# A decoder step on one core: cached keys turned in place by VectorE, two key buffers in turn, scores on 32x32 tiles

## The reference

```python
def dilated_attention_sample(q, k_new, v_new, cache_k, cache_v, rel_bias):   # cache: (8, 2048, 12, 64)
    kc = concatenate([cache_k, k_new], axis=1); vc = concatenate([cache_v, v_new], axis=1)
    for w, d in ((128, 1), (512, 4), (2048, 16)):
        idx = n_past + arange(n_new)[:, None] - arange(w // d + 1)[None, :] * d
        kg, vg = kc[:, idx], vc[:, idx]
        logits = einsum('bthe,btjhe->bhtj', q, kg) * 64 ** -0.5 + bias[bucket(j * d)]
        p, s, lse = softmax_stats(logits, idx >= 0)
        o = einsum('bhtj,btjhe->bthe', p, vg) / s
    return merge_branches(outs, lses)        # branches weighted by their softmax denominators
```

## Time and profile before

| | |
|---|---|
| median of 3 runs | 1428.6 us (1427.8 to 1431.9) |
| the profiled execution, timed | 1427.6 us |
| its span, first to last instruction | 1425.7 us |
| mean granted TensorE clock | 0.985 of 2.4 GHz |
| busy: TensorE, VectorE, ScalarE | 97%, 36%, 17% |
| DMA over the span | 524.8 MB, 368 GB/s |

### The profile page before, as it was taken

The page is one execution under the profiler, slowest core; times in us unless marked ns, Lnnn a source line. Parts: engine busy times, 40 slices in busy tenths (PEclk is TensorE's granted clock), DMA queues, the critical chain, the costliest instruction groups (busy, mean ns, idle before and its releaser), DMA issues.

```text
span 1425.7 us, 22384 instructions
## 1 busy us (share of the span) xinstructions
PE 1378.0 (97%) x7929; PEld 585.1 (41%) x7930; DVE 519.1 (36%) x1159; ACT 242.8 (17%) x432; POOL 24.3 (2%) x45
## 2 busy tenths in 40 slices
PE   5999999999989999999999999999999999999996
PEld 2655666665453333333333333333333333333332
DVE  2211356554674232333233332323332332323325
ACT  0001334443021111111111111111111111111111
POOL 0000000000030000000000000000000000000000
PEclk9999999999979999999999999999999999999998
DMA  9959457999948999999999988999999999998981
GB/s 361 372 204 350 174 182 304 417 419 379 349 142 319 399 422 418 427 426 424 427 427 426 426 364 371 414 425 427 425 425 425 428 426 425 424 425 322 419 346 37
DMA packets 62917, 524.78 MB, mean 368 GB/s; under 512 B 8732, under 2 KB 10325, under 8 KB 22762
## 3 DMA queue, kind: packets, MB, share of 16 engines
q1 hardware_dynamic: 58896, 517.61, 88.5%
q0 software_dynamic: 2160, 5.96, 1.2%
q10 hardware_dynamic: 1834, 0.84, 0.3%
HBM read 520.92 MB, written 3.46 MB: 368 GB/s over the span
## 4 chain that ended last, share of the span: by engine, by line
PE 81%; DMA 11%; issue 4%; DVE 2%; SPq 1%; ACT 0%; ACTq 0%; DVEq 0%; POOLq 0%
PE ps L1845 29%; PE ps L1925 14%; PE ps L1361 6%; DMA arena<-in_w_up 6%; PE ps L1783 5%; DMA arena<-in_cache_v 4%; PE ps L1737 3%; PE ps L1424 3%; PE ps L1652 3%; PE ps L1837 2%; PE ps L1594 2%; PE ps L1421 2%; PE ps L1741 2%; PE ps L1855 2%; DMA arena<-by_distance 1%
## 5 line engine op out<-in xcount | busy, mean ns | idle before, releaser
L1845 PE MATMUL ps<-arena 128*64 128x512 f32 x2048 | 451.3, 598 | 3.3 <-DMA arena<-in_w_up 3.3
L1845 PEld LDWEIGHTS ps<-arena 128*64 128x64 f32 x2048 | 144.3, 138 | 308.1 <-issue 300.2
L1925 PE MATMUL ps<-arena 128*64 128x512 f32 x1024 | 226.8, 595 | 0.1
L1361 PE MATMUL ps<-arena 128*128 128x128 f32 (+4 forms) x1071 | 151.8, 283 | 19.5 <-DVE arena L784 10.8
L1281 DVE TENSOR_SCALAR arena<-ps 128x512 f32<-128x512 f32 (+1 forms) x35 | 24.2, 691 | 367.6 <-PE ps L1845 306.1
L1361 PEld LDWEIGHTS ps<-arena 128*128 128x128 f32 (+4 forms) x1071 | 116.6, 144 | 82.4 <-issue 48.2
L1925 PEld LDWEIGHTS ps<-arena 128*64 128x64 f32 x1024 | 70.9, 137 | 150.2 <-issue 150.2
L727 ACT ACTIVATE arena<-arena 128x512 f32<-128x512 f32 (+1 forms) x35 | 22.1, 631 | 443.6 <-DVE arena L1281 443.6
L1216 DVE TENSOR_TENSOR arena<-arena,ps 128x512 f32<-128x512 f32 x32 | 22.1, 690 | 192.6 <-PE ps L1774 192.6
L1424 PE MATMUL ps<-arena 128*128 128x320 f32 x288 | 82.8, 439 | 1.9 <-DMA arena<-in_w_in 1.9
L1783 PE MATMUL ps<-arena 64*128 64x512 f32 x288 | 79.7, 637 | 0.0
(11 more groups left out here) (264 smaller groups left out, 979.8 us busy)
## 6 DMA issues: line engine op xcount, KB each, us to landing
arena<-in_w_up SPq DMA_DIRECT2D x128, 2048.0 KB, 15.7
arena<-in_w_down SPq DMA_DIRECT2D x128, 1024.0 KB, 13.5
arena<-in_w_ada SPq DMA_DIRECT2D x12, 2048.0 KB, 17.4
arena<-in_cache_k SPq DMA_DIRECT2D x16, 1536.0 KB, 14.4
arena<-in_cache_v SPq DMA_DIRECT2D x16, 1536.0 KB, 9.6
arena<-in_w_in SPq DMA_DIRECT2D x6, 2048.0 KB, 23.4
arena<-in_cache_k SPq DMA_DIRECT2D x32, 192.0 KB, 12.5
arena<-in_cache_v SPq DMA_DIRECT2D x32, 192.0 KB, 10.5
```

Source lines behind the costliest of these rows:

```text
L1361: return nc.tensor.transpose(o, i, ident[0:n, 0:n])
L1845: ins = mm(bank(part)[64 * h:64 * h + 64], xe_t[:, 0, at:at + 64], up_w[:, k, FF * part + 512 * h:FF * part + 512 * h + 512], start=False, ...
L1925: ins = mm(bank(3)[64 * h:64 * h + 64], a_t[:, 0, at:at + 64], dn_w[:, kk, 512 * h:512 * h + 512], start=kk == 0, stop=kk == KC - 1)
```

## The change

VectorE transposes the keys in place: one `transpose` of a part of the buffer turns each 32x32 square by itself (10 blocks x 24 squares along a partition). A square then holds 32 of the 64 values of a head in its partitions and 32 keys along them. TensorE multiplies 32x32 tiles: for each of 24 groups of 32 values and each of 4 quarters of the partitions, one product of 32 rows, 32 columns and 320 keys; four quarters go to four banks (0 to 3), three groups of heads to three column tiles. `q_wide` holds the queries for this, each at the partitions of all four quarters; they come from `q_rep`, made once by 16 small products with the identity (`qr_done`) and four copies on ScalarE (`qr_ready`). The scores of the new keys go to bank 4 as before, by `qbd`. The 60 transposes of a batch on TensorE, their 18 copies, and `kt_sb` are gone; in its place lies a second key buffer (`k_buf[0]`, `k_buf[1]`).

The keys of batch 0 are turned one block at a time at steps 4 to 13 of the loop over the prompt's heads, those of batch 1 around the table of biases, those of batch b+2 in `dve_batch` of b.

```diff
-        k_sb = view(KX, KB, DA)
...
-        kt_sb = view(KTX, AC, NCACHE)
+        k_buf = [view(KX, KB, DA), view(KTX, KB, DA)]
+        MX = KTX + KB * DA
+        FG = DA // 32
+        q_wide = view(MX, FG, 32)
...
+        q_rep = view(P, FG, NTOK - SEQ)
...
-            load_keys(ck, slice(1, 2), 0)
+            sp.wait_ge(proj_done, len(UNITS))
+            load_keys(1)
             sp.wait_ge(out_kv, 96)
             sp.wait_ge(sb_done, 1)
             sp.dma_start(wo_sb, wo_d).then_inc(wo_in, 16)
-            load_keys(ck, slice(2, 3), 1)
+            sp.wait_ge(s_done, 1)
+            load_keys(2)
             for b in range(1, NB - 1):
+                if b < NB - 2:
+                    sp.wait_ge(s_done, b + 1)
+                    load_keys(b + 2)
                 load_values(slice(b, b + 1), b)
-                if b < NB - 2:
-                    load_keys(ck, slice(b + 2, b + 3), b + 1)
...
+            act.wait_ge(vec_out, 64)
+            act.wait_ge(qr_done, 1)
+            for g in range(4):
+                ins = nc.scalar.copy(q_rep.rearrange("p (c g) t -> p g c t", g=4)[:, g],
+                                     bank(3 + g, 0, AC * 64).rearrange("p (c t) -> p c t", c=AC))
...
+            def turn_keys(par, js):
+                part = k_buf[par][:, js, :].rearrange("p j d -> p (j d)")
+                return v_.transpose(part, part)
+            def turn_group(par, group, times):
+                dve.wait_ge(k_low_in[par][group] if group < 2 else k_high_in[par], times * (16 if group < 2 else 64))
+                turn_keys(par, slice(4 * group, min(4 * group + 4, KB))).then_inc(k_ready, 1)
...
+            v_.memset(q_wide, 0.0)
...
+                for m in range(4):
+                    ins = v_.tensor_copy(wide[:, :, m, :, 8 * m:8 * m + 8],
+                                         q_rep.rearrange("p (j m h) t -> p j m h t", j=3, m=4)[:, :, m, :, own])
...
-            queries(slice(SEQ, SEQ + NS))
-
+            dve.wait_ge(qr_ready, 1)
+            queries(slice(SEQ, SEQ + NS), slice(0, NS))
+            turn_group(1, 0, 1)
             dve.wait_ge(sb_done, 1)
...
             mean_squares(0)
+            turn_group(1, 1, 1)
+            turn_group(1, 2, 1)
...
-                V(v_.tensor_tensor_reduce(prob[0:96, 0:NCACHE], ps[0:96, 0:NCACHE], s_bias[0:96, 0:NCACHE], 1.0, -3e38,
-                                          ALU.add, ALU.max, st[0:96, 12:13]))
-                V(v_.tensor_reduce(st[0:96, 13:14], prob[0:96, NCACHE:NCACHE + 64], AX.X, ALU.max))
+                for a in range(4):
+                    ins = v_.tensor_tensor_reduce(blocks[0][:, :, a], bank(a, 0, 32 * KB)[0:96].rearrange("p (j k) -> p j k", k=32),
+                                            blocks[1][:, :, a], 1.0, -3e38, ALU.add, ALU.max, st[0:96, 18 + a:19 + a])
+                V(ins)
+                V(v_.tensor_reduce(st[0:96, 22:23], prob[0:96, NCACHE:NCACHE + 64], AX.X, ALU.max))
+                V(v_.tensor_reduce(st[0:96, 12:13], st[0:96, 18:23], AX.X, ALU.max))
...
+                if turns:
+                    turn_group(par, 0, times)
                 dve.wait_ge(st_done, b * 3 + 2)
...
+                if turns:
+                    turn_group(par, 1, times)
+                    turn_group(par, 2, times)
...
+            dve_batch(NB - 2, 0, 0, False, True, False)
             inverse_roots(0)
...
+            def cached_scores(keys):
+                for n in range(FG // 3):
+                    for a in range(4):
+                        for j in range(3):
+                            f, rows = FG // 3 * j + n, slice(32 * a, 32 * a + 32)
+                            ins = mm(bank(a, 0, 32 * KB)[32 * j:32 * j + 32].rearrange("p (j k) -> p j k", k=32),
+                               q_wide[rows, f, :], keys[rows, :, 32 * f:32 * f + 32], start=n == 0, stop=n == FG // 3 - 1,
+                               tile_position=(32 * a, 32 * j))
```

More of the change, by code:

```diff
@@ L412, in _ @@
             sp.dma_start(query_sum[0:96], t["query_sum"].rearrange("p (a b) -> p a b", a=3)).then_inc(hot_in, 16)
-            def load_keys(cache, b, before):
-                for half in range(2):
-                    sp.wait_ge(kt_done, before * 18 + AC * half + AC)
-                    load_low(cache, k_sb, b, half, k_low_in[half])
-                sp.wait_ge(kt_done, before * 18 + 3 * AC)
-                load_high(cache, k_sb, b, k_high_in)
             def load_values(b, used):
@@ L969, in _, with queries @@
             V(v_.memset(place[:, CAP:128], -0.5))
-            def queries(cols):
+            def queries(cols, own):
                 for par in range(2):
@@ L1094, in dve_batch @@
                 if not first:
                     mask_output(b - 1)
-                if more:
-                    dve_turned(0, b + 1)
-                if not first:
                     keep_output(b - 1)
-                if more:
-                    dve_turned(1, b + 1)
-                    dve_turned(2, b + 1)
-                if first:
-                    queries(slice(SEQ + NS, SEQ + 2 * NS))
+                if turns:
+                    turn_group(par, 0, times)
                 dve.wait_ge(st_done, b * 3 + 2)
@@ L1557, in sums_of_squares @@
                 ins.then_inc(ss_done, 1)
+            pe.wait_ge(proj_act, len([w for w in UNITS if w[3] == "act"]))
+            for g in range(4):
+                for a in range(0, 128, 32):
+                    ins = mm(bank(3 + g, 0, AC * 64)[a:a + 32].rearrange("p (c t) -> p c t", c=AC),
+                             ident[:, 32 * g:32 * g + 32], q_t[:, :, SEQ:NTOK], start=True, stop=True, tile_position=(0, a))
+            ins.then_inc(qr_done, 1)
             pe.wait_ge(hot_in, 64)
@@ L1606, in output_sample, with pe_batch @@
                 ins.then_inc(wo_done, 1)
-            def pe_batch(b, first, more):
+            def pe_batch(b, par, first, more):
                 pe.wait_ge(qbd_ready, b + 1)
                 pe.wait_ge(s_max, b + 1)
-                pe.wait_ge(kt_dve, b * 9 + 10)
-                pe.wait_ge(kt_act, b * 9 + 10)
-                scores(bank(0), lambda c: kt_sb[:, c, 0:512])
-                scores(bank(1), lambda c: kt_sb[:, c, 512:1024])
-                scores(bank(2, 0, 256), lambda c: kt_sb[:, c, 1024:NCACHE])
-                scores(bank(2, 256, 320), lambda c: k_t[:, c, SEQ:NTOK]).then_inc(s_done, 1)
+                pe.wait_ge(k_ready, b * 3 + 3)
+                scores(bank(4, 0, 64), lambda c: k_t[:, c, SEQ:NTOK])
+                cached_scores(k_buf[par]).then_inc(s_done, 1)
                 if not first:
                     values(b - 1)
-                if more:
-                    keys(0, b + 1)
-                else:
+                if not more:
                     pe.wait_ge(og_ready, 1)
@@ L1627, in pe_batch @@
                     heads_apart(b - 1)
-                if more:
-                    keys(1, b + 1)
-                    keys(2, b + 1)
                 if not first:
```

156 lines of the change are left out of this document (50 added, 106 removed).

## The result

The changed kernel takes 1440.6 us (median; 1436.6 to 1443.1), against 1428.6 before: ratio 1.0074, interval 1.0059 to 1.0088. It is 0.7% slower, where 1423.0 was forecast. Its profiled execution has a span of 1441.4 us, the one of before 1425.7.

The account below looks back on a forecast made before the run. It took DMA to bound the loop, 18.5 us a turn, TensorE's 18.1 close behind. 8.1 us earlier at the stream's end less 2.5 for the clock gave 5.6: 1427.6 to 1422.0, median 1.0 above, 1423.0 us; range 1417 to 1436.

Parts of the forecast that it names:

- What bounds the kernel: Loop over sample batches: DMA takes 18.5 us a turn, TensorE 18.1; two limits nearly meet, DMA's the later.
- Step 1: Time until the first scores: they begin at 209.6 against 213.79, 4.2 us earlier, with VectorE last.
- Step 2: Turning keys on VectorE: 8.8 us a batch, VectorE's turn 13.6 us, under DMA's 18.5.
- Rival (b): VectorE becomes the bound in the turns: 14 to 27 us lost, less 8, about 1441 us; 9%.
- Step 3: Scores on 32x32 tiles: 4.5 us, 4.8 with the new keys, as before, if row tiles overlap.
- rival (c): Row tiles don't overlap in the scores: 18 us of scores, TensorE's turn 25 us, 1475 us; 4%.
- Step 4: Loads in the ramp: values 1 issued at 231.5, 8 us earlier; values 2 land 6.3 us earlier.
- Turns: Sample batches' loop: DMA-bound turns of 18.5 us in a dense queue of loads.
- rival (a): Clock falls every turn, `values` behind the wait over 7 us: up to 18 + 5 us against 8.1, 1436 at two thirds; 12%.
- step 6: TensorE's clock after 6 to 7 us idle each turn: 2.5 us lost in all, mostly hidden; granted clock 0.9 and more.
- Step 5: End of the load stream: values 6 need only the buffer, landing at 338.5 against 346.6, 8.1 us earlier.
- The last doubt: Unseen wait ahead of the loads: keys b+3 behind `s_done`, itself behind VectorE's maximum and turning; no size given.

Follow-up runs that it names:

- before_split: Kernel before, with the values' buffer given back and the next values requested in three parts; 1427.8 us, ratio 0.9980.
- fill_wait_b7: Changed kernel plus 32 filling identity products on TensorE ahead of each wait for values; 1435.6 us, ratio 1.0039 to the kernel before.
- split_values: Changed kernel, values' buffer given back and next values requested in three parts; 1433.0 us, ratio 1.0016 to the kernel before.
- split_late_squares: Changed kernel with the three-part values request and group 0's sums of squares moved behind the first scores; 1431.0 us, ratio 1.0018 to the kernel before.
- split_fill_more: Changed kernel with the three-part values request and 24 filling products per wait, none ahead of the last values; 1429.6 us, ratio 1.0001 to the kernel before.
- all_three: Changed kernel with three-part values request, 24 filling products and sums of squares behind the first scores; 1429.8 us, ratio 1.0007 to the kernel before.
- values_first: Changed kernel, values of b requested ahead of keys b+2, VectorE's turning one batch later; 1455.5 us, ratio 1.0184 to the kernel before.

## Why the prediction was wrong, step by step

It was wrong: 1423.0 forecast, 1440.6 measured, past the range's upper end of 1436. For the landing of values 6 it said 338.5 and 359.18 was found, 20.7 us later, of which 3.05 are chance.

- **What bounds the kernel.** "DMA's is the later one" was right for the kernel before, but as a statement on bandwidth alone. There is a third limit, the closed loop of the single values buffer: product, issue, transfer. At full clock it is 4.5 (to block 9) + 2.9 + 10.3 = 17.7 us, the last two being means of the five turns from values 1 to 6, and only 0.8 us under the 18.5 of the transfers. The prediction didn't compute it. A late request held the kernel before back a little as well: the waits of `values` for their loads there, 2.2 us in five turns, are gone in before_split, which changes the request alone, and its turns are TensorE's 18.1 us. That this is under the 18.5 of the transfers, for five turns, isn't explained by a run.
- **Step 1, first scores.** Forecast 209.6, 4.2 us earlier; found 214.83, less chance 211.8, and the 32x32 part is reached 1.7 to 3.3 us earlier than in the profile of before, counted from H (over all traces 69.1 to 70.7 us, those with the sums moved left out, against 72.4 to 74.0 for the old scores: 3.7 us in the mean). The term that failed is "only the last heads remain, some 3 us, so 194.5": `q_rep` began at 200.37. Less chance that is 197.3, and 2.8 us late. The last heads are a chain across three engines, not TensorE's work less the transposes. TensorE, not VectorE, came last ahead of the first scores (table, then the sums, end at 214.90), which took some of this back. `q_rep` (2.81 for 2.7) and the table (8.06 for 8.0) were right.
- **Step 2, turning.** 3.38 + 5.01 = 8.4 us a batch for 8.8; right. Rival (b) falls. The estimate of 7.5 us, scaled by width from the 311 ns of the Trainium skill, "VectorE: DVE Perf Modes", section "The three transpose paths", doesn't hold here: 3072 columns took 3.38, 1.1 ns a column. No run here turns 128x128 in bf16.
- **Step 3, scores.** 4.94 us at full clock for 4.5; 0.4 short, but right in kind. Row tiles overlap, rival (c) falls. Missing was what the 384 instructions in one piece bring, stops of 0.9 to 2.6 us at the first passage.
- **Step 4, the ramp.** Values 1 were to be asked for at 231.5 and were at 240.20. Of the 8.7 us 3.05 are chance, 2.2 the later start of the scores, 2.5 the stop, and 1.4 the second scores at half clock (5.88 for 4.5), together a little more than was lost. They landed 18.5 us after the request instead of 15.9. In the old order keys 3 stood behind values 1; now they stand ahead, and only 4.5 us of their 9.25 have passed when values 1 are asked for. From the issue of keys 3 it is 22.8 to 24.4 us until `values` of batch 1 start, in the changed kernel (22.97), fill_wait_b7, split_values, split_late_squares, split_fill_more and all_three. The prediction had this term, but counted on the 8 us as won to pay for it.
- **Turns.** 18.5 forecast, 19.95 found in the four from values 1 to 5: 5.8 us. This is rival (a), whose mark ("that product takes over 7 us") was met in five of six waits (6.9 to 8.0). The sentence that failed stands in step 6: "one or two microseconds behind each idle stretch, mostly hidden". The loss in the product was 1.8 to 2.9 us, so only little above it; what could hide it was 0.8 us a turn, not the 2 that were taken from the bandwidth alone.
- **Step 5, the end.** 17.0 us forecast from values 5 to 6, 20.7 found: the product to block 9 7.45 instead of 5.1, request to landing 13.2 instead of 11.75. Then 2.8 us more in the product of values 6, whose time is wholly on the path. The gain by order, a last turn shorter than the others, didn't show in the changed kernel at all; it shows with the split request: 16.8 in split_values, 14.3 in split_fill_more.
- **Step 6, the clock.** Forecast 0.9 and more in a turn, found 0.83 to 0.85. The Trainium skill, "TensorE: Matmul & The Clock Gate", section "HAM oscillation", was right where I overruled it: the product behind each wait started cold in every turn here (7.3 for 5.1 us). The trace differs from its words in one thing: the burst, 13.9 to 14.2 us of TensorE's work in a turn, was longer than the wait of 4.9 us, not shorter. The upper price that I drew from it, 18 + 5 us, didn't come: taking most of the low clock away gave 5 us of the whole with the filling's own cost in it (fill_wait_b7), and moving the request gave 8 with the clock left low. Rival (a) had the right mechanism at 12%, and the time it gave, 1436, was still short, since the ramp's loss came on top.
- **The last doubt**, keys of b+3 behind `s_done`, wasn't the cause. They were asked for 4.5 to 5.4 us ahead of each landing, so a shortage of keys held nothing up.

The +4.9 us of V0 to V1 are mainly the order's doing: in values_first, where values 1 stand ahead of keys 3, they landed 17 us behind V0, with second scores as slow as in the changed kernel (5.61 us). fill_wait_b7 has 19.35 there only because its filling stands ahead of V0. In V6 to V7 the changed kernel loses its slow product; in split_values, all_three and split_fill_more, whose values 6 take 5.08 us, TensorE waits 1.3 to 2.8 us for values 7 instead. What stays open: how much the half clock still costs once the request is split.

## What to carry to other kernels

Where a buffer is single, add up its closed loop (use, issue of all its DMAs, transfer) beside the bandwidth and each engine's work; the smallest distance between these decides how much a slower product may cost. Work taken from an engine that the transfers bound becomes idle time, which brings the low clock in the very product that the next request waits for. The cheap edit is to give the buffer back in parts: it won back 8.3 of the changed kernel's 10.6 us (by the ratios) and improved the old kernel by 0.2%.
